# A two-block transformer kernel: the slabs ahead of two norms run their last two banks together, and three norm hand-overs are reordered

## What is computed

```
def rmsnorm(x, g):
    return x * rsqrt(mean(x * x, axis=-1) + EPS) * g

x = x + mix @ w_out                                   # first block, mix_out
h2 = rmsnorm(x, ln2)
x = x + square(relu(h2 @ w_mlp1)) @ w_mlp2            # mlp_up, mlp_down
h3 = rmsnorm(x, ln3)
x = x + sigmoid(h3 @ w_pg) * (p @ w_pp)               # ple_gate, ple_p
x = rmsnorm(x, ln_f)
h = rmsnorm(x, pre_norm_g_2[0])                       # even layer
u = h @ w_in_ab_2                                     # lstm_q is its first slab
...
x = x + rmsnorm(y, post_norm_g_2[0])                  # y = even_out
h = rmsnorm(x, pre_norm_g_2[1])                       # odd layer
u = h @ w_in_c_2                                      # odd_z is its first slab
...
```

## Time and profile before

| what | value |
|---|---|
| median of 3 runs | 2011.26 us (2011.19 to 2011.35) |
| profiled execution | 2011.68 us |
| its span, first to last instruction | 2010.0 us |
| TensorE busy in it | 1955.4 us (97%) |
| VectorE, ScalarE, GpSimd busy | 761.4, 780.0, 844.5 us (38%, 39%, 42%) |
| mean granted TensorE clock | 0.992 of full |

### The profile page before, as it was taken

How to read it: one execution, slowest core, us unless ns; L and a number is a source line. 1 busy time by engine, 2 the same in 40 slices (tenths; PEclk the granted TensorE clock), 3 DMA queues, 4 the chain that set the end, 5 groups by cost and what they waited for, 6 DMA issues and landing times.

```text
span 2010.0 us, 25558 instructions
## 1 busy us (share of the span) xinstructions
PE 1955.4 (97%) x9220; PEld 1623.9 (81%) x9220; DVE 761.4 (38%) x1202; ACT 780.0 (39%) x1525; POOL 844.5 (42%) x654
## 2 busy tenths in 40 slices
PE   7999999999999999999999999999999999999898
PEld 5777888998888888888888788888787778888787
DVE  4211321340124232222337864212477636025743
ACT  5322443413324333333365333253456535333332
POOL 3523444425254445444354443344333344445452
PEclk9999999999999999999999899999999999999999
DMA  4522333313133323333232232233222232333231
GB/s 141 147 68 61 102 84 89 84 42 105 52 112 99 126 88 107 103 95 98 74 105 74 70 99 64 63 94 91 62 74 69 68 131 69 101 93 94 85 105 53
DMA packets 98873, 177.99 MB, mean 89 GB/s; under 512 B 10779, under 2 KB 16551, under 8 KB 98780
## 3 DMA queue, kind: packets, MB, share of 16 engines
q1 hardware_dynamic: 94212, 170.17, 29.0%
q10 hardware_dynamic: 4568, 6.56, 1.1%
HBM read 172.75 MB, written 3.93 MB: 88 GB/s over the span
## 4 chain that ended last, share of the span: by engine, by line
PE 59%; issue 20%; DVE 9%; POOL 8%; ACT 3%; POOLq 0%; ACTq 0%; DVEq 0%
PE proj L1809 19%; PE proj L1811 18%; PE proj L1810 18%; POOL w_lo L581 8%; DVE arena L1684 1%; DVE arena L1682 1%; DVE arena L1791 1%; ACT arena L868 1%; PE work L1944 1%; PE proj L2282 1%; DVE arena L1681 0%; DVE arena L1685 0%; PE work L2327 0%; ACT arena L1056 0%; ACT arena L1057 0%
## 5 line engine op out<-in xcount | busy, mean ns | idle before, releaser
L581 POOL TENSOR_TENSOR w_lo<-w_raw,w_hi 128x512 fp32r<-128x512 f32 x632 | 839.1, 1346 | 1137.6 <-ACT w_hi L606 997.8
L1809 PE MATMUL proj<-act_hi,w_hi 128*128 128x512 f32 (+1 forms) x1328 | 505.0, 380 | 7.7 <-DVE arena L1740 2.0
L606 ACT CAST w_hi<-w_raw 128x512 fp32r<-128x512 f32 x536 | 313.7, 620 | 483.1 <-PE proj L1811 458.6
L1810 PE MATMUL proj<-act_lo,w_hi 128*128 128x512 f32 (+1 forms) x1328 | 498.6, 375 | 0.0
L1811 PE MATMUL proj<-act_hi,w_lo 128*128 128x512 f32 (+1 forms) x1328 | 498.4, 375 | 0.0
L1809 PE MATMUL proj<-w_hi,act_hi 128*128 128x512 f32 x800 | 321.1, 401 | 7.5 <-DVE arena L1776 4.9
L1811 PE MATMUL proj<-w_hi,act_lo 128*128 128x512 f32 x800 | 313.4, 392 | 0.0
L1810 PE MATMUL proj<-w_lo,act_hi 128*128 128x512 f32 x800 | 313.1, 391 | 0.0
L1809 PEld LDWEIGHTS proj<-act_hi,w_hi 128*128 128x128 f32 x1328 | 251.3, 189 | 58.3 <-issue 5.6
L1811 PEld LDWEIGHTS proj<-act_hi,w_lo 128*128 128x128 f32 x1328 | 251.3, 189 | 45.5
L1810 PEld LDWEIGHTS proj<-act_lo,w_hi 128*128 128x128 f32 x1328 | 251.4, 189 | 44.0 <-issue 0.5
(11 more groups left out here) (308 smaller groups left out, 1791.9 us busy)
## 6 DMA issues: line engine op xcount, KB each, us to landing
w_raw<-in_w_in SPq DMA_DIRECT2D x154, 256.0 KB, 2.9
w_raw<-in_w_in_ab SPq DMA_DIRECT2D x146, 256.0 KB, 2.7
w_raw<-in_w_mlp SPq DMA_DIRECT2D x128, 256.0 KB, 2.8
w_raw<-in_w_in_c SPq DMA_DIRECT2D x64, 256.0 KB, 2.8
w_raw<-in_w_out_ab SPq DMA_DIRECT2D x32, 256.0 KB, 2.7
w_raw<-in_w_out_c SPq DMA_DIRECT2D x32, 256.0 KB, 2.9
w_raw<-in_w_o_gla SPq DMA_DIRECT2D x16, 256.0 KB, 2.9
w_raw<-in_w_out SPq DMA_DIRECT2D x16, 256.0 KB, 2.7
```

The source lines that it names most:

```text
L581: return pool.tensor_tensor(w_lo[:, slot, :], w_raw[:, slot, :], w_hi[:, slot, :].bitcast(F32), ALU.subtract)
L606: act.copy(w_hi[:, b % RING, :], w_raw[:, b % RING, :]).then_inc(hi_ready, 1)
L1809: pe.matmul(out_, a_hi, b_hi, start=first, stop=False)
L1810: pe.matmul(out_, a_hi, b_lo, start=False, stop=False)
```

## The change

`slab_by_bank` becomes `slab_by_banks`, which takes groups of banks. With `ONE_BY_ONE` it is the old order. With `LAST_TWO` bank 0 runs alone, then bank 1, then banks 2 and 3 together, block by block; `block_used` is given behind each block of that last group. `mix_out[1]` and `ple_gate[1]` use `LAST_TWO`; `even_out1[1]` and `odd_out1[1]` stay one by one. On `ln2` and `pre0` the transposes, the casts and the work on VectorE are put in another order: tiles 0 and 1 one after the other, tiles 2 and 3 side by side. On `pre1` only the numbers in ScalarE's `prepare` calls change.

```diff
@@ ScalarE, ln2
-            for m in range(MT):
-                own_root(x, s, m)
-                prepare(up0.first + (0, 0, 2, 8)[m])
-                if m:
-                    token_hi("ln2", m - 1, s)
-                prepare(up0.first + (0, 0, 6, 8)[m])
-            token_hi("ln2", MT - 1, s)
+            own_root(x, s, 0)
+            token_hi("ln2", 0, s)
+            own_root(x, s, 1)
+            prepare(up0.first + 4)
+            token_hi("ln2", 1, s)
+            prepare(up0.first + 7)
+            own_root(x, s, 2)
+            own_root(x, s, 3)
+            prepare(up0.first + KD)
+            token_hi("ln2", 2, s)
+            token_hi("ln2", 3, s)
@@ ScalarE, pre0
+            token_hi("pre0", 0, second)
             embedding_gate(second, 1, MT + 1)
-            token_hi("pre0", 0, second)
             q0 = by_name["lstm_q"][0]
+            prepare(q0.first + 3)
+            token_hi("pre0", 1, second)
+            prepare(q0.first + 7)
             embedding_gate(second, 2, MT + 2)
-            prepare(q0.first + 2)
-            token_hi("pre0", 1, second)
-            prepare(q0.first + 5)
             embedding_gate(second, 3, MT + 3)
             prepare(q0.first + KD)
@@ ScalarE, pre1
                 own_root(y, s, m)
-                prepare(z0.first + (0, 0, 2, 7)[m])
+                prepare(z0.first + (0, 0, 3, 8)[m])
                 if m:
                     token_hi("pre1", m - 1, s)
+                prepare(z0.first + (0, 0, 4, 8)[m])
                 next_root(m)
-                prepare(z0.first + (0, 0, 5, 8)[m])
+                prepare(z0.first + (0, 0, 8, 8)[m])
@@ VectorE, ln2 (normed_ln2 is the scale and the norm of one tile)
-            for m in range(MT):
-                add_to_x(mixes[1], 1, m)
-                if m:
-                    token_lo("ln2", m - 1)
-                step(token_scale("ln2", tile(m)))
-                normed("ln2", m, x, rstd[:, m:m + 1], ln2_row)
-            token_lo("ln2", MT - 1)
+            add_to_x(mixes[1], 1, 0)
+            normed_ln2(0)
+            add_to_x(mixes[1], 1, 1)
+            token_lo("ln2", 0)
+            normed_ln2(1)
+            token_lo("ln2", 1)
+            add_to_x(mixes[1], 1, 2)
+            add_to_x(mixes[1], 1, 3)
+            normed_ln2(2)
+            normed_ln2(3)
+            token_lo("ln2", 2)
+            token_lo("ln2", 3)
@@ VectorE, pre0
-            for m in range(MT):
+            for m in range(2):
                 embedded(1, m)
-                if m:
-                    token_lo("pre0", m - 1)
-                if m == MT - 1:
-                    token_lo("pre0", m)
+                final_gain(1, m)
+                token_lo("pre0", m)
+            for m in (2, 3):
+                embedded(1, m)
+            for m in (2, 3):
+                token_lo("pre0", m)
+            for m in (2, 3):
                 final_gain(1, m)
@@ TensorE
+            def slab_by_banks(s, pair, groups, before=None):
+                for group in groups:
+                    for j in range(s.n):
+                        if before:
+                            before(group[0], j)
+                        if group is groups[0]:
+                            pe.wait_ge(lo_ready, s.first + j + 1)
+                        ...
+                        for c in group:
+                            if j == 0 and s.need[c]:
+                                pe.wait_ge(proj_free, s.need[c])
+                            ...
+                            if j == s.n - 1:
+                                ins.then_inc(proj_full, 1)
+                        if group is groups[-1] and j < s.n - 1:
+                            ins.then_inc(block_used, 1)
+            ONE_BY_ONE, LAST_TWO = ((0,), (1,), (2,), (3,)), ((0,), (1,), (2, 3))
...
-            slab_by_bank(by_name["mix_out"][1], "act", before=early_tiles("ln2", [(2, 1), (3, 1), (3, 7)]))
+            slab_by_banks(by_name["mix_out"][1], "act", LAST_TWO, before=early_tiles("ln2", [(1, 7), (2, 4)]))
-            features_by_half(ups[0], "ln2", late_tiles("ln2", [4]))
+            features_by_half(ups[0], "ln2", late_tiles("ln2", [4, 6]))
-            slab_by_bank(by_name["ple_gate"][1], "act", before=early_tiles("pre0", [(2, 3), (3, 1), (3, 6)]))
+            slab_by_banks(by_name["ple_gate"][1], "act", LAST_TWO, before=early_tiles("pre0", [(1, 6), (2, 3)]))
-                if (half, j) == (0, 3):
-                    turn_tokens("pre0", MT - 1)
+                if half == 0 and j in (3, 5):
+                    turn_tokens("pre0", 2 + (3, 5).index(j))
```

More of the change, by code:

```diff
@@ L1415, in _, with normed_ln2 @@
             vec.wait_ge(ln2_row_loaded, 16)
-            for m in range(MT):
-                add_to_x(mixes[1], 1, m)
-                if m:
-                    token_lo("ln2", m - 1)
+            def normed_ln2(m):
                 step(token_scale("ln2", tile(m)))
                 normed("ln2", m, x, rstd[:, m:m + 1], ln2_row)
-            token_lo("ln2", MT - 1)
+            add_to_x(mixes[1], 1, 0)
[10 more added lines that the diff above has]
+            token_lo("ln2", 3)
             ups, downs = by_name["mlp_up"], by_name["mlp_down"]
@@ L1847, in slab @@
                     slab_block(s, j, kind, pair, k0 + j, tokens, wait_bank)
[L1849 to L1854, removed]
+            def slab_by_banks(s, pair, groups, before=None):
+                assert [c for group in groups for c in group] == list(range(s.banks))
+                for group in groups:
                     for j in range(s.n):
                         if before:
-                            before(c, j)
-                        if c == 0:
+                            before(group[0], j)
+                        if group is groups[0]:
                             pe.wait_ge(lo_ready, s.first + j + 1)
-                            if ready:
-                                pe.wait_ge(ready[0], ready[1] + j + 1)
                         slot = (s.first + j) % RING
                         hi, lo = tile_of(pair)(j)
[L1864 to L1868, removed]
+                        for c in group:
+                            if j == 0 and s.need[c]:
+                                pe.wait_ge(proj_free, s.need[c])
+                            t = natural(c)
+                            ins = three(proj[:, c, :], hi[:, t], lo[:, t], w_hi[:, slot, :], w_lo[:, slot, :], j == 0, j == s.n - 1)
+                            if j == s.n - 1:
+                                ins.then_inc(proj_full, 1)
+                        if group is groups[-1] and j < s.n - 1:
                             ins.then_inc(block_used, 1)
+            ONE_BY_ONE, LAST_TWO = ((0,), (1,), (2,), (3,)), ((0,), (1,), (2, 3))
             def features_by_half(s, name, before):
@@ L2205, in _, with last_tiles @@
             slab(by_name["ple_gate"][0], "tokens", ready=ready_act("ln3"))
-            slab_by_bank(by_name["ple_gate"][1], "act", before=early_tiles("pre0", [(2, 3), (3, 1), (3, 6)]))
-            def last_tile(half, j):
-                if (half, j) == (0, 3):
-                    turn_tokens("pre0", MT - 1)
+            slab_by_banks(by_name["ple_gate"][1], "act", LAST_TWO, before=early_tiles("pre0", [(1, 6), (2, 3)]))
+            def last_tiles(half, j):
+                if half == 0 and j in (3, 5):
+                    turn_tokens("pre0", 2 + (3, 5).index(j))
                 elif (half, j) == (1, 6):
@@ L2216, in last_tile @@
                     ins.then_inc(r_row_full, 1)
-            features_by_half(by_name["lstm_q"][0], "pre0", last_tile)
+            features_by_half(by_name["lstm_q"][0], "pre0", last_tiles)
             narrow_slab(by_name["lstm_if"][0], 0)
@@ L2344, in _ @@
             slab(by_name["even_out1"][0], "tokens", ready=ready_act("yb"), before=turn(sb_o, act_ready, ACT_AT["yb"]))
-            slab_by_bank(by_name["even_out1"][1], "act", before=early_tiles("pre1", [(2, 3), (3, 1)]))
+            slab_by_banks(by_name["even_out1"][1], "act", ONE_BY_ONE, before=early_tiles("pre1", [(2, 3), (3, 1)]))
             features_by_half(by_name["odd_z"][0], "pre1", late_tiles("pre1", [1, 6]))
@@ L2361, in _ @@
             slab(by_name["odd_out1"][0], "tokens", pair="aux", ready=(aux_ready, AUX_AT["mixb"]))
-            slab_by_bank(by_name["odd_out1"][1], "aux")
+            slab_by_banks(by_name["odd_out1"][1], "aux", ONE_BY_ONE)
 _INS = ["x", "p", "ln1", "w_in", "w_a2", "b_a", "gla_gn", "w_o_gla", "w_o_attn", "w_out", "ln2", "w_mlp1", "w_mlp2",
```

## The result

The changed kernel takes **2015.8 us** (median of 20 runs, 2013.3 to 2020.4) beside 2011.5 us for the kernel before (20 runs on the same chip, 2009.2 to 2014.3). The ratio is 1.0022, 95% interval 1.0016 to 1.0028: slower by 4.4 us, 3.2 to 5.6. Forecast were 2018.3, slower, in a range of 2010.0 to 2020.8. Sign and range held; the forecast is 2.5 us too high, +7.0 where the runs show +4.4, and the range, 10.8 us wide, was more than twice the effect.

The account below looks back on a forecast made before the run. TensorE, busy for 97% of the span, bounds the kernel, so only its waits or lower clock count. Terms -2.5 + 2.4 + 1.9 + 5.2 = +7.0 us on the median 2011.3 gave 2018.3 us, range 2010.0 to 2020.8.

Parts of the forecast that it names:

- ln2, -2.5: At ln2, TensorE's two waits for tile 2's normed halves, 1.29 and 1.23 us, go: -2.5 us.
- pre0, +2.4: At pre0, tile 0's earlier turn makes a 3.8 us wait (+3.4); tile 3's wait goes (-1.3), lstm_if adds 0.3.
- tile 3's wait: At pre0, TensorE's wait for tile 3 before 1078.65 goes, its turn being just in time: -1.3 us.
- pre1, +1.9: At pre1, two casts ahead of tile 2's second root lengthen TensorE's wait for bank 3's add from 2.2 to 4.1 us.
- The clock, +5.2: Behind the new waits at pre0 and pre1, a fall to clock 0.50 each, middle price: +5.2 us, bounds 0 and 9.2.
- The three runs before, all within 0.16 us though they hold three falls, don't show such scatter: Argument against the first rival: if falls came by execution, runs would scatter between 2013 and 2018.
- No wait over 2.9 us in the rows was spared: Argument against the first rival: the trace's three waits of 2.9 us and more were each followed by clock 0.50.
- Behind `lstm_dec`, 0: In the stage behind lstm_dec, no change of time was forecast: 0.
- the delays weren't taken up later: Rival: pre0's and pre1's delays vanish in later waits, leaving 2008.8 us; chance 0.06.
- the wait for `lstm_dec` stayed 3.5: Rival: the chain behind lstm_if is freed from GpSimd, the 3.5 us wait and its fall go: 2010.2 us; chance 0.06.
- tile 0 wasn't ready: Rival: at pre0 tile 0's second half is ready at 1057.6, stage -1.7 instead of +2.4: 2011.6 us; chance 0.04.
- The first rival: New waits cost no clock (2013.1 us, chance 0.12) or only one does (middle 2015.7 us, chance 0.19).

Follow-up runs that it names:

- busy_waits: The changed kernel plus 32 superfluous transposes in each of TensorE's waits at pre0 and for bank 3 at pre1; 2011.7 us, ratio 1.0003.
- pre0_tile0_later: pre0_only with tiles 0 and 1 turned at blocks 1 and 4 of banks 2 and 3 taken together; 2012.05 us, ratio 1.0004.
- casts_ahead: Kernel before with only the two casts moved ahead of tile 2's second root at pre1, the number behind it unchanged; 2015.0 us, ratio 1.0019.
- casts_behind: pre1_only with its two casts ahead of tile 2's second root taken back behind it; 2012.1 us, ratio 1.0006.
- pre1_only: Kernel before with only the change's numbers in pre1's prepare calls; 2015.2 us, ratio 1.0016.
- three_waits_less: Kernel before with the change's ln2 part, pre0's last tile a block later, pre1's bank 3 add ahead of tile 2's scalings; 2005.0 us, ratio 0.9971.
- before_busy: Kernel before plus 30 unread transposes in the wait for lstm_dec and 44 in that ahead of odd_out0; 2007.8 us, ratio 0.9985.
- pre0_only: Kernel before with only the pre0 part of the change; 2017.4 us, ratio 1.0033.
- busy_too: three_waits_less plus the same filler transposes as before_busy at the same two waits; 2002.3 us, ratio 0.9958.

## Why the prediction held, and where it was off

- **ln2, -2.5:** read -2.9, and no wait took its place. Tile 2 was ready sooner than the step said, since GpSimd had a gap. 0.25 us more than the two waits went at tile 3, whose eight transposes took 1.04 us between starts before and take 0.79 now.
- **pre0, +2.4:** the new wait was 3.9 (forecast 3.8), tile 3's wait went as forecast (-1.3), L1491 ended the new one, and without a fall the stage costs +2.3 (busy_waits). That it is the time of the request, and not the grouping, was argued from VectorE's row; pre0_tile0_later shows it.
- **pre1, +1.9:** read +1.9, by the two steps named, the later root and the dear pair. casts_ahead and casts_behind show that the two casts ahead of the root do it all.
- **The clock, +5.2:** the mechanism held, and the profiled execution shows +5.0 for the two falls. In the median run this term is mis-sized: it measured 4.1 (busy_waits), and a fall behind the same wait is of 6.8 us in one trace and of 3.4 in another.
- **"The three runs before, all within 0.16 us though they hold three falls, don't show such scatter":** this sentence failed. Twenty runs of the kernel before lie between 2009.2 and 2014.3.
- **"No wait over 2.9 us in the rows was spared":** true of the one trace read, and too clean. The shortest of those three waits, 2.9 us at L2316, was followed by a fall in eight of the twelve profiled executions here and by none in pre1_only, casts_ahead, three_waits_less and before_busy. And the waits of 2.2 to 2.5 us at pre1 and ln2, free of it in the profile read, brought a fall of 3.4 us in other executions (pre0_only and casts_behind; pre1_only and casts_ahead), worth 1.6 and 1.2 us by starts. So the old waits already cost some clock in the median run, which the sum put at nothing.
- **Behind `lstm_dec`, 0:** read -1.4, a shorter fall in that one execution. Executions of the unchanged stage show 10.2, 6.8 and 3.4 us there, so this is scatter and not the change.
- The rivals: the delays weren't taken up later (the difference at the end of pre1 is that at the end of the kernel, within 0.4 us), the wait for `lstm_dec` stayed 3.5, and tile 0 wasn't ready. The first rival has a part of the truth in the scatter. That the median, 2015.8, lies on its number for one fall, 2015.7, is an accident: the profiled execution has both falls.
- Luck: the sum of the profiled execution, +5.4, is nearer to +4.4 than the forecast because a fall of 10.2 us behind `lstm_dec` was one of 6.8 there. And the range held by its width; the clock term alone was known to no better than 0 to 9.2.
- Of the rows, the prediction names three crosswise: its at ln2 are rows 2, its there are rows 3, and its at pre0 are rows 4. The bracket of L1194 stands in none of them; in the trace it is 1.18 us, at 635.99. The readings themselves are right.

What stays open: why the median came out 2.5 us under the forecast is settled only in part. The smaller price of the new falls gives 1.1 us, and the larger win at ln2 0.4; the rest may be the clock that the old waits cost, but one trace of each kernel doesn't size that. And no run tells which part of the new order at ln2 wins there, the two banks together or the later turns.

## What to carry to other kernels

A piece of work that TensorE is to turn or take should be placed by the time at which the other engine writes it, not by the time at which its bank is full: at pre0 3.4 us too early cost 5.3 us, and two entries of one table gave them back. What stands ahead of a releasing root or of a bank's release counts at once, and three casts behind the root cost nothing that the runs show; the bank's add went first in the version that beat both. And where the clock falls behind waits, it costs from half to more than the wait's own length again (by the prediction's estimate 1.4 us behind 2.9 and 4.6 behind 3.5; by starts 2.6 behind the new wait of 3.9), and three runs within 0.2 us are no measure of the scatter.

## What was not expected of the hardware

- The runs of one kernel spread over 5 us (the kernel before, 0.25%) to 7 us (the changed one) with the waits unchanged. The stretch at 0.50 near 30 us was of 3.4, 6.8 or 10.2 us, and TensorE came to ln2 up to 1.6 us sooner or 2.1 us later for it than in the kernel before. The lengths of the stretches at clock 0.50 behind one and the same wait were 3.4, 6.8 or 10.2 us in different executions, and those that began behind ln2's and pre1's waits of 2.2 to 2.5 us, and behind the one of 2.9 us, came in some and not in others.
- Transposes that nothing reads held the clock at 1.00: 32 of them in a wait of 3.9 us left no fall behind it, nor did 44 in the wait of 5.0. With 30 of them and then twenty multiplications of 4 columns, 1.7 us long, the clock fell once (before_busy) and stayed once (busy_too).
- A pair of VectorE instructions costs 1.4, 2.3 to 2.4 or 3.3 to 3.5 us for the same work, by where GpSimd's pieces lie when it starts.
